# Modulation weights loaded in two halves, and the context shift added as products of a repeated column

## The reference

```python
def modulation(cond, w_mod, b_mod):
    m = jax.nn.silu(cond) @ w_mod + b_mod
    return jnp.split(m, 6, axis=-1)

def modulate(x, g, shift, scale):
    return rmsnorm(x, g) * (1.0 + scale) + shift

    sh1, sc1, g1, sh2, sc2, g2 = modulation(c, ...)            # latent tokens
    csh1, csc1, cg1, csh2, csc2, cg2 = modulation(c_ctx, ...)  # context tokens
    h_lat = modulate(x, g_attn, sh1, sc1)
    h_ctx = modulate(ctx, g_attn, csh1, csc1)
    z = h @ w_in        # 1184 columns, split among the heads
```

## Time and profile before

| what | value |
|---|---|
| time, median of 3 runs | 1366.46 us (1365.99 to 1366.98) |
| time of the profiled execution | 1368.26 us |
| its span, first to last instruction | 1366.3 us |
| PE, PEld busy | 1322.1 us (97%), 1117.9 us (82%) |
| DVE, ACT, POOL busy | 1022.2 us (75%), 737.3 us (54%), 510.9 us (37%) |
| mean granted clock of TensorE | 0.991 |

### The profile page before, as it was taken

The page is one execution under the profiler, slowest core; times in us unless marked ns, Lnnn a source line. Parts: engine busy times, 40 slices in busy tenths (PEclk is TensorE's granted clock), DMA queues, the critical chain, the costliest instruction groups (busy, mean ns, idle before and its releaser), DMA issues.

```text
span 1366.3 us, 19011 instructions
## 1 busy us (share of the span) xinstructions
PE 1322.1 (97%) x7118; PEld 1117.9 (82%) x7118; DVE 1022.2 (75%) x1396; ACT 737.3 (54%) x1405; POOL 510.9 (37%) x350
## 2 busy tenths in 40 slices
PE   4899998999999999999999999999999999999998
PEld 0688887889888988898888888888888888888886
DVE  1888777787788777776687796767687776868678
ACT  2756565788877877984223543444353535344440
POOL 2567664021199995411000031404123232404333
PEclk8999999999999999999999999999999999999999
DMA  9565657633156564401334535527261735437053
GB/s 375 181 179 167 176 162 236 200 91 88 27 214 194 154 206 153 107 16 32 93 108 139 174 103 213 189 94 265 83 236 62 250 121 213 157 125 245 31 185 124
DMA packets 149130, 210.55 MB, mean 154 GB/s; under 512 B 10136, under 2 KB 101144, under 8 KB 146224
## 3 DMA queue, kind: packets, MB, share of 16 engines
...
q0 software_dynamic: 256, 0.05, 0.0%
...
## 4 chain that ended last, share of the span: by engine, by line
PE 73%; DVE 15%; ACT 7%; DMA 2%; issue 1%; SPq 0%; DVEq 0%; ACTq 0%
PE f_ps L2749 19%; PE f_ps L2712 17%; PE a_ps L1449 7%; PE o_ps L1797 6%; PE a_ps L1465 5%; PE a_ps L1495 5%; PE f_ps L2280 5%; ACT s_pr L1546 3%; DVE s_nmx L1631 2%; PE t_ps L977 2%; DMA t_wm<-in_w_mod 1%; PE t_ps L966 1%; PE f_ps L2765 1%; PE t_ps L992 1%; DVE f_fin L2557 1%
## 5 line engine op out<-in xcount | busy, mean ns | idle before, releaser
L2260 POOL TENSOR_TENSOR f_wr<-f_wr,f_wr 128x1024 f32<-128x1024 f32 x24 | 61.8, 2576 | 286.1 <-DMA f_wr<-in_w_mlp 157.3
L2749 PE MATMUL f_ps<-f_bh,f_ah 128*128 128x512 f32 x392 | 152.6, 389 | 0.6 <-DVE mix L2583 0.6
L2749 PE MATMUL f_ps<-f_bh,f_al 128*128 128x512 f32 x392 | 152.5, 389 | 0.0
L2749 PE MATMUL f_ps<-f_bl,f_ah 128*128 128x512 f32 x392 | 152.5, 389 | 0.0
L1645 DVE TENSOR_TENSOR l_pT<-a_ps,l_pT 128x512 fp32r<-128x512 f32 (+1 forms) x192 | 109.0, 594 | 53.2 <-ACT l_pT L1556 53.1
L2581 DVE TENSOR_TENSOR mix<-mix,f_ps 128x512 f32<-128x512 f32 x180 | 116.5, 682 | 37.5 <-PE f_ps L2749 37.2
L1449 PE MATMUL a_ps<-l_k,l_q 96*128 96x512 f32 (+1 forms) x576 | 136.4, 366 | 0.5 <-DVE l_mo L1657 0.5
L977 PE MATMUL t_ps<-w_in,t_h 128*128 128x416 f32 (+2 forms) x600 | 123.8, 352 | 0.0
L1556 ACT ACTIVATE l_pT<-a_ps 128x512 fp32r<-128x512 f32 (+1 forms) x192 | 95.0, 525 | 39.6 <-PE a_ps L1465 39.2
L1563 ACT ACTIVATE l_pr<-a_ps,l_nb 128x256 f32<-128x256 f32 (+1 forms) x128 | 100.5, 790 | 12.5 <-DVE l_nb L1636 10.2
L1449 PEld LDWEIGHTS a_ps<-l_k,l_q 96*128 96x128 f32 x576 | 95.3, 189 | 12.5 <-DVE l_mo L1657 0.7
...
## 6 DMA issues: line engine op xcount, KB each, us to landing
f_hq<-scratch_hs SPq DMA_DIRECT2D x64, 512.0 KB, 5.4
...
f_ring<-scratch_hs SPq DMA_DIRECT2D x32, 512.0 KB, 5.2
f_wr<-in_w_mlp SPq DMA_DIRECT2D x24, 512.0 KB, 3.8
...
```

Of the source, the lines that this page charges most:

```text
L2749: last = nc.tensor.matmul(ps[:, b, :], op_a[s][x][:, f, t * P:(t + 1) * P], op_b[s][w][:, f, :], start=(i in (M1, M2, M5) and f == 0 and k ...
```

## The change

The 8 MB of modulation weights are loaded in other pieces, each of 256 rows and 1024 columns (1 MB): four of scale first, then the first context tile, `a0`, `a1`, the second context tile and the norms' gains, then four of shift. PE makes the scale rows from the first four (16 products), spreads the two context halves, and projects tile 0 without its shift. After that it makes the shift rows (16 products), turns the shift row of the context into a column per 128 values (`turn_shift`, four transposes), ACT and DVE take the high and low part of these 8 columns (`t_shift_col`), and PE adds `shift @ w_in` to the accumulating bank: `shift_rows`, 24 products with one column repeated 128 times as the weights. Tile 1 is projected the same way, with its own `shift_rows`. So the two additions of DVE for tile 0 and POOL's addition for tile 1 go, and so do two of the eight spreads with two copies. The four latent spreads stay. Both tiles still read the same `w_in`. On ACT, `high_weights("a1")` and the square of tile 1 now stand behind the two `hi_fill` of tile 0.

The diff, with context left out (places in memory, semaphore counts and the waits of the spent ones are cut):

```diff
@@ -144,8 +144,10 @@
     zs = room("t_z", [P, IN_W])
-    wm_in = {i: Z.room(at, skip)(f"t_wm{i}", [P, n, 2 * D]) for i, at, skip, n in ((0, "H", 0, 4), (4, "L", 0, 3), (7, "T", 9984, 1))}
-    wm = [wm_in[i][:, k - i, :] for k in range(KC) for i in (0, 4, 7) if 0 <= k - i < (4, 0, 0, 0, 3, 0, 0, 1)[i]]
+    wm_scale = Z.room("H")("t_wm_scale", [P, KC, D])
+    wm_near = Z.room("L")("t_wm_near", [P, KC - 2, D])
+    wm_far = Z.room("T", 9984)("t_wm_far", [P, 2, D])
+    wm_shift = lambda k: wm_near[:, k, :] if k < KC - 2 else wm_far[:, k - KC + 2, :]
...
@@ -262,7 +265,7 @@
-    spread_bank = (5, 6, 7, 3, 4, 5, 6, 7)
+    spread_bank = (5, 7, 4, 5, 6, 7)
...
@@ -285,6 +288,10 @@
         return w_kv[i][:, :] if j == "kv" else w_uq[i][:, :, :]
+
+    def shift_view():
+
+        return ps[:, UB, 0:4 * 64].rearrange("p (c j r) -> p j c r", c=4, j=2)[:, :, :, 1]
...
@@ -338,8 +345,8 @@
-        def load_wm(k):
-            sp.dma_start(wm[k], A["w_mod"][0, k * P:(k + 1) * P, 0:2 * D]).then_inc(wm_loaded[k], 16)
+        def load_pair(n, cols, dst):
+            sp.dma_start(dst, A["w_mod"][0, 2 * (n % 4) * P:2 * (n % 4 + 1) * P, cols].rearrange("(k p) c -> p k c", p=P)).then_inc(wm_loaded[n], 16)
...
@@ -347,16 +354,16 @@
         sp.dma_start(ident[:, :], A["ident"]).then_inc(ident_loaded, 16)
-        for k in range(KC - 2):
-            load_wm(k)
+        for n in range(4):
+            load_pair(n, slice(D, 2 * D), wm_scale[:, 2 * n:2 * n + 2, :])
         load_x(0)
-        load_wm(KC - 2)
-        load_wm(KC - 1)
         load_raw("a0")
+        load_raw("a1")
         load_x(1)
-        load_raw("a1")
         sp.dma_start(norms[:, :], A["norm_rows"]).then_inc(gains, 16)
+        for n in range(4):
+            load_pair(4 + n, slice(0, D), wm_near[:, 2 * n:2 * n + 2, :] if n < 3 else wm_far[:, :, :])
...
@@ -404,11 +411,9 @@
             pool.wait_ge(h_scaled, t)
-            if t == 1:
-                pool.wait_ge(spread_copied, 4)
             if t == NCT:
-                pool.wait_ge(spread_copied, 8)
-            shift = shift_l if lat(t) else shift_c
+                pool.wait_ge(spread_copied, 6)
+            shift = shift_l
...
@@ -487,7 +492,7 @@
                 widen_key(i - 1)
-            if i + 1 < NT and i != 1:
+            if 1 < i < NT - 1:
...
@@ -513,7 +518,7 @@
             if j == "a0":
-                act.wait_ge(wm_used, 4)
+                act.wait_ge(wm_used, KC)
...
@@ -526,11 +531,9 @@
-            dst = (scale_l, shift_l)[n % 2] if n >= 4 else (scale_c, shift_c)[n % 2]
-            f = n // 2 % 2
+            dst = scale_c if n < 2 else (scale_l, shift_l)[n % 2]
+            f = n if n < 2 else n // 2 - 1
             act.wait_ge(spread, n + 1)
-            if n < 4:
-                act.wait_ge(h0_ready, n // 2 + 1)
...
@@ -637,13 +640,15 @@
         high_weights("a0")
-        square_x(1, stx[:, 1:2])
-        high_weights("a1")
         hi_fill("x1", 0)
+        high_weights("a1")
+        copy_spread(0)
+        copy_spread(1)
+        square_x(1, stx[:, 1:2])
         root_x(1)
-        for n in range(4):
-            copy_spread(n)
+        act.wait_ge(turned_shift, TURNED0 + 1)
+        nc.scalar.activation(shift_col[0][:, :].rearrange("p (j c) -> p j c", j=2), shift_view(), ACT.Copy).then_inc(shift_hi, 1)
...
@@ -721,11 +726,9 @@
                 x = xr[:, 0, f * BANK:f * BANK + BANK]
-                dve.wait_ge(spread, 2 * f + 1)
-                link(V.scalar_tensor_tensor(out=x, in0=x, scalar=stx[:, 0:1], in1=ps[:, spread_bank[2 * f], :],
-                                            op0=ALU.mult, op1=ALU.mult))
-                dve.wait_ge(spread, 2 * f + 2)
-                V.tensor_tensor(x, x, ps[:, spread_bank[2 * f + 1], :], ALU.add).then_inc(h0_ready, 1)
+                dve.wait_ge(spread, f + 1)
+                V.scalar_tensor_tensor(out=x, in0=x, scalar=stx[:, 0:1], in1=ps[:, spread_bank[f], :],
+                                       op0=ALU.mult, op1=ALU.mult).then_inc(h0_ready, 1)
...
@@ -859,16 +862,21 @@
         link(V.tensor_scalar_add(bg[64:P, 0, :], bg[64:P, 0, :], 1.0))
+        dve.wait_ge(wm_used, KC)
+        link(V.tensor_tensor(mo[64:P, :], ps[64:P, UB, :], bm[64:P, :], ALU.add))
+        V.tensor_tensor(mo[64:P, :], mo[64:P, :], gm[64:P, :], ALU.mult).then_inc(mod_ready, 1)
         inverse_x(0)
-        dve.wait_ge(wm_used, KC)
-        link(V.tensor_tensor(mo[:, :], ps[:, UB, :], bm, ALU.add))
-        V.tensor_tensor(mo[:, :], mo[:, :], gm, ALU.mult).then_inc(mod_ready, 1)
         lo_fill("x1", 0)
+        low_weights("a1")
         inverse_x(1)
-        low_weights("a1")
         scale_x(1)
+        dve.wait_ge(wm_used, 2 * KC)
+        V.tensor_tensor(mo[0:64, :], ps[0:64, UB, :], bm[0:64, :], ALU.add).then_inc(mod_ready, 1)
+        dve.wait_ge(shift_hi, HI0 + 1)
+        V.tensor_tensor(shift_col[1][:, :].rearrange("p (j c) -> p j c", j=2), shift_view(),
+                        shift_col[0][:, :].rearrange("p (j c) -> p j c", j=2).bitcast(F32), ALU.subtract).then_inc(shift_lo, 1)
...
@@ -942,8 +950,10 @@
                 f = int(kind[1])
-                if t:
-                    pe.wait_ge(h_ready, t + (f if t == NCT else 1 if t > NCT else 0))
+                if t == 1:
+                    pe.wait_ge(h_scaled, 1)
+                elif t:
+                    pe.wait_ge(h_ready, 1 + f if t == NCT else t)
...
@@ -975,10 +985,13 @@
                     ins = MM(ps[:, ZB + n % 2, 0:w], hT[a][:, k, :], w_in[x][:, k, ZC[c]],
-                             start=(k == 0 and i == 0), stop=(k == KC - 1 and i == 2))
+                             start=(k == 0 and i == 0), stop=(k == KC - 1 and i == 2 and t != 1))
                     fill(*between[k])
-            ins.then_inc(z_ready, 1)
+            if t == 1:
+                shift_rows(n)
+            else:
+                ins.then_inc(z_ready, 1)
...
@@ -1006,28 +1019,21 @@
-        pe.wait_ge(silu_ready, 1)
-        for k in range(KC):
-            pe.wait_ge(wm_loaded[k], 16)
-            for j in range(4):
-                last = MM(ps[32 * j:32 * j + 32, UB, :], silu[:, k, :], wm[k][:, j * BANK:(j + 1) * BANK],
+        def modulation(k, js, w):
+            for j in js:
+                last = MM(ps[32 * j:32 * j + 32, UB, :], silu[:, k, :], w[:, j % 2 * BANK:(j % 2 + 1) * BANK],
             last.then_inc(wm_used, 1)
-        pe.wait_ge(ident_loaded, 16)
-        pe.wait_ge(mod_ready, 1)
-            r, j = 1 - n // 4, (2, 0, 3, 1)[n % 4]
-            if n >= 5:
-                pe.wait_ge(spread_copied, n - 4)
-            MM(ps[:, spread_bank[n], :], ident[:, 32 * j + r:32 * j + r + 1].to_broadcast([P, P]), mo[:, :],
+            r, j = 1 if n < 2 else 0, (2, 3, 2, 0, 3, 1)[n]
+            if n in (3, 5):
+                pe.wait_ge(spread_copied, n // 2)
+            rows = slice(64 * (j // 2), 64 * (j // 2) + 64)
+            MM(ps[:, spread_bank[n], :], ident[rows, 32 * j + r:32 * j + r + 1].to_broadcast([64, P]), mo[rows, :],
-        for n in range(4):
-            spread_row(n)
-        fill("x0", 0)
-        fill("x1", 0)
...
@@ -1040,16 +1046,46 @@
                     pe.wait_ge(w_lo, 1)
-                ins = MM(ps[:, ZB, 0:NA], hT[0][:, k, :], w_in[1][:, k, 0:NA], start=False, stop=(k == KC - 1))
+                MM(ps[:, ZB, 0:NA], hT[0][:, k, :], w_in[1][:, k, 0:NA], start=False, stop=False)
+
+        def turn_shift():
+
+            for c in range(4):
+                last = nc.tensor.transpose(ps[:, UB, 64 * c:64 * c + 64], mo[0:64, c * P:(c + 1) * P], ident[0:64, 0:64])
+            last.then_inc(turned_shift, 1)
+
+        def shift_rows(n):
+
+            pe.wait_ge(shift_lo, LO0 + 1)
+            for k in range(KC):
+                for i, (a, x) in enumerate(((0, 0), (0, 1), (1, 0))):
+                    ins = MM(ps[:, ZB + n % 2, 0:NA], shift_col[a][:, k:k + 1].to_broadcast([P, P]), w_in[x][:, k, 0:NA],
+                             start=False, stop=(k == KC - 1 and i == 2))
+        pe.wait_ge(silu_ready, 1)
+        for k in range(KC):
+            pe.wait_ge(wm_loaded[k // 2], 16)
+            modulation(k, (2, 3), wm_scale[:, k, :])
+        pe.wait_ge(ident_loaded, 16)
+        pe.wait_ge(mod_ready, 1)
+        spread_row(0)
+        spread_row(1)
+        fill("x0", 0)
+        fill("x1", 0)
         project_first()
+        for k in range(KC):
+            pe.wait_ge(wm_loaded[4 + k // 2], 16)
+            modulation(k, (0, 1), wm_shift(k))
+        pe.wait_ge(mod_ready, 2)
+        turn_shift()
+        shift_rows(z_at(0))
             if i == 0:
-                for n in range(4, 8):
+                for n in range(2, 6):
...
@@ -1057,7 +1093,7 @@
                     pe.wait_ge(w_lo, JOBS.index("kv"))
-                    pe.wait_ge(spread_copied, 8)
+                    pe.wait_ge(spread_copied, 6)
```

15 lines of the change are left out of this document (8 added, 7 removed).

## The result

The changed kernel took 1371.62 us in the median of five executions (1370.14 to 1374.40), the kernel before 1366.46 beside it (1365.99 to 1368.33): a ratio of 1.0038, with a 95% interval of 1.0026 to 1.0049. That is 5.2 us lost, inside the range and twice the forecast's 2.5. The profiled execution took 1371.36, its span 1368.5 at a mean granted clock of 0.997; against the span of the execution shown of before, 1366.3, it lost 2.2, close to the sum (in time it lost 3.1, since 2.9 us of this execution lie outside its span and 2.0 of the one before). So there are two questions: whether the sum's steps are there, and where the other 3 us come from.

A forecast was written before the change was run, and what follows sets the result against it. Waits are mostly PE's; the early stretch follows weight loads, then ACT, DVE and PE, with DVE the bound from tile 1 on. +2.7 less 0.3, rounded to +2.5, on the 1366.46 median gives 1369.0 us; range 1366.3 to 1372.5.

The forecast's parts named there:

- the sum: New date for DVE's step on tile 1's `t_c`: 60.8 instead of 58.11, +2.7, less 0.3, so +2.4, rounded to 2.5.
- The scale half: Start of the kernel: scale products end at 17.2, a two-tile step takes 0.86, tile 0's first product at 22.8.
- The shift half: After tile 0's first projection: shift products end at 34.6, z of tile 0 is copied at 41.4 instead of 43.85.
- What sets tile 1's start: ACT's four copies of the latent spreads, last from 44.85, set tile 1's first product at 48.1, 1.9 earlier than 49.99.
- Tile 1's second set: 24 more products behind tile 1's projection, 4.6 us of PE that nothing hides; its z copied at 57.6, not 54.92.
- What comes back: DVE's two r parts run without POOL's table work beside them and give back 0.3 us.
- The rival in which DVE's `w_uq` pair gives the loss back: DVE between 58 and 77 us: its 3.96 us pair might shorten, returning 2.2; +0.2, 1366.7; chance 0.15.
- The rival in which the products are hidden: Tile 1's shift products cost nothing, leaving the 1.9 us gain and DVE's: 1364; chance 0.06.
- tile 1's date is the whole kernel's: What tile 1 wins or loses at DVE's step (58.11 before), the whole kernel wins or loses; nothing later waits for absolute time.
- 2.5 on the median is 1369.0: Whole kernel: the 2.5 us loss is added to the median of the kernel before, 1366.46, giving 1369.0.
- the slower rival: PE's clock drops at its pauses or PE falls behind in the first projection: +4.5 to +5.5, about 1371.5; chance 0.27.
- PE now works over half of that time, which speaks against it: Argument against a clock drop at PE's 1.7 us bias pause and around tile 0's turning: PE is busier than before.

The follow-up runs named there:

- e5: The kernel before, run again with no edit for a second trace: 1366.57 us, ratio 1.000.
- e10: Kernel before plus full-width products nobody reads, behind its last five modulation steps, to keep TensorE busy: 1365.39 us, 0.9989 of the kernel before.
- e1: The changed kernel run again with no edit: 1371.46 us, 1.0036 of the kernel before.
- e9: The change plus four full-width products nobody reads, filling TensorE's first pause (waiting for bias and gain): 1371.01 us, 1.0032 of the kernel before.
- e6: The change plus narrow filling products for TensorE's two pauses; those for the first ran beside the scale steps, leaving that pause: 1372.23 us, 1.0041.
- e2: The change without tile 1's 24 shift products, so its shift is missing from z: 1368.82 us, 1.0009 of the kernel before.
- e3: The change with tile 1's 24 shift products issued twice: 1375.35 us, 1.0072 of the kernel before.
- e11: The change with tile 1's shift added by DVE from two more spreads, first pause filled by four full-width products: 1367.90 us, 1.0008 of the kernel before.
- e4: The change with tile 1's shift added by DVE from two more spreads instead of 24 products: 1369.41 us, 1.0018 of the kernel before.
- e7: The version of e4 plus the narrow filling products of e6: 1370.04 us, 1.0022 of the kernel before.
- e8: The version of e7 with the six spreads behind tile 0 also reordered: 1370.10 us, 1.0022 of the kernel before.

## Why the forecast was half right

Three dates of each trace, with its span, put the terms in order:

| execution profiled | clock | z of tile 0 | first product of tile 1 | t_c of tile 1 | span |
|---|---|---|---|---|---|
| before, as shown | 0.991 | 43.85 | 49.99 | 58.11 | 1366.3 |
| before again (e5) | 0.991 | 42.45 | 48.59 | 56.70 | 1364.5 |
| before, filled (e10) | 0.996 | 40.41 | 46.82 | 55.04 | 1362.4 |
| the change | 0.997 | 41.76 | 47.88 | 60.56 | 1368.5 |
| the change again (e1) | 0.992 | 45.40 | 51.57 | 64.25 | 1372.0 |
| the change, filled (e9) | 0.995 | 42.30 | 48.42 | 61.10 | 1369.2 |

**The scale half: right.** Ended 17.50 for 17.2; a step of two column tiles took 0.89 (5.34 for six) where 0.86 was taken, so half a step's work was indeed not half its time. First product at 23.26 for 22.8, first projection done at 28.14 for 27.6.

**The shift half: right.** Last step done at 35.14 for 34.6; the last load is in by 33.7 or so where TensorE is seen waiting for it (e6, e9), a microsecond after the 32.5 of the text, which cost nothing in the change's trace, where the step at 33.25 did not wait. From there to the first shift product 1.71 for 2.1, with ACT's copy and DVE's subtraction at 0.18 and 0.17, the lower of the two bounds. z of tile 0 at 41.76 for 41.4.

**What sets tile 1's start: the right date for a reason half wrong.** The text let ACT's four copies set it, and held the last of them (44.85) by the end of the spreads (44.8). The copies are in the chain, but the spreads are not what starts them. Now of 64 rows each, the spreads took 1.99 instead of 3.59 and ended at 43.58, and that brought nothing: ACT's rows have no idle time from the copy of tile 0's z at 41.76 through the fourth copy at 44.66 to the high part of `t_c` at 45.13, and TensorE idles 1.53 ahead of 45.81 for DVE's `t_c` behind it. From the copy of tile 0's z to tile 1's first product it is 6.12 in the change and 6.14 in the kernel before (43.85 to 49.99) and again in e5, 6.17 in e1; only in e10, where the fourth copy did wait 0.17 for a spread, it is 6.41. So ACT's own list from tile 0's z on sets it, and z of tile 0 is the date to forecast. That the spreads' end gave nearly the same date was luck. POOL's addition was rightly given nothing.

**Tile 1's second set: right.** 4.72 in the row, 4.8 at `t_c` by e2's trace and 4.8 in the times by e3. z of tile 1 at 57.37 for 57.6, `t_c` at 60.56 for 60.8.

**What comes back: right.** The pair of r parts gave 0.32 for 0.3. The rival in which DVE's `w_uq` pair gives the loss back fell (3.97). The rival in which the products are hidden fell with e2 and e3. That tile 1's date is the whole kernel's held too: from `t_c` of tile 1 to the end of the span it is 1307.4 to 1308.2 us in all six rows of the table.

**The number: the step "2.5 on the median is 1369.0" failed.** The 2.5 was worked out against one execution, which took 1368.26, and in which the clock was low in the bursts and the spreads; then it was put on the median of others, 1366.46. Made against its own time the same sum gives 1368.26 + 2.5 = 1370.8, and the profiled execution took 1371.36. e5 shows 1.4 us of it at `t_c` and 1.8 in the span; the rows stood in the text (a spread of 6.28 where the next took 3.59), and nobody asked whether every execution had them. In the medians, 3.8 of the 5.2 us stand in the executions of the change at 0.996 and above too (1370.3); the other 1.4 is what its executions at a lower clock add. So the median fell near the slower rival's 1371.5 by the sum of two things, of which that rival had one.

**The slower rival was given too little: "PE now works over half of that time, which speaks against it" failed.** Four of ten executions have a mean clock of 0.993 or less, and in the one of them that was profiled (e1) the clock fell all the same, at the pause named, with 3.7 us as its price; in two more, at 0.994, there seems to be a part of it. Half speed was priced at 2 to 3 us; and with four to six of ten executions it deserved nearer half the chances than 0.27.

**The loss with the clock up at the start** is the plainest reading of the change: e9 against e10, 5.6 us in the medians and 6.06 at `t_c` of tile 1. Of these 4.7 are the second set, and 1.6 stand at tile 1's first product already (48.42 against 46.82). e11, without the second set, starts tile 1 still later (49.59) and keeps 2.7 us of loss at `t_c`. The change moves work behind the last modulation load, and it moves that load itself: its last piece is used from 33.8 where it was from 26.1, for x of tile 1, the gains and the raw weights of a0 and a1 now go ahead of it. TensorE waited only 0.16 us for it in e9, so its own work up to there takes as long; how the 1.6 divides between the two was not tested. The advance of 2.1 us that the changed kernel showed at tile 1's first product against the earlier trace rows was none against a kernel before with its clock up: e10 has that product 1.1 us ahead of the change's. What is left open is why a pause of 1.7 us is followed by the lower clock in some executions and not in others of the same program. One thing in the rows ahead of it does differ. Here are the scale steps of the change, and below them those of e1:

```profile
7.61 7.32 PE L1024 MATMUL t_ps<-t_wm_scale,silu 128*32 128x512 f32 x24 [7.61 <-DMA t_wm_scale<-in_w_mod]
```

```profile
7.41 9.94 PE L1024 MATMUL t_ps<-t_wm_scale,silu 128*32 128x512 f32 x32 [7.41 <-DMA t_wm_scale<-in_w_mod]
```

In the change 24 products are done in 7.32 us and the last 8 wait for their load; in e1 more of them are long, and all 32 follow each other for 9.94. All the traces of versions that begin like the change begin with products of 1.06 us (though the windows give a clock of 1.00 for them) and go over to 0.59. In the three in which the clock fell at about 20 us (e1, e2, e3) the first step began at 7.41 to 7.50, and the products between 12 and 13 us still took 0.81 to 1.01 us in the median; in the six that kept it there (the change, e4, e6, e7, e9, e11), two of them with the pause filled, it began at 7.58 or later, and these products took 0.59 to 0.64. e8 began late too (7.87, 0.59), kept it at 20 and lost it at 21.6. So an execution that goes over to the short products later was more likely to lose the clock at the pause; that is an order seen in ten traces and not a cause shown. That the pause takes part is supported by the counts under e11, from few executions.
